# Gating the attention output in three groups, and a fifth pair of weight places for the output projection

## The chip, the cores and the metric

The kernel runs on 1 core of one Trainium2 chip. The metric is the device time of one execution in microseconds (us); lower is better. Engines are named as the profile names them: PE (TensorE) does the matmuls, ACT (ScalarE) and DVE (VectorE) the elementwise work, POOL (GpSimd) and SP (SyncE) little else than issuing DMAs. Each engine works through its own queue strictly in order and waits at semaphores for the others.

## What is computed

Three transformer-like blocks in a row over 256 tokens of 1024 features, all float32. The first block ends in a mixture of 16 experts, whose weights must be streamed from memory. The change concerns the second block, two layers of gated attention:

```python
def second_block(x, norm_g, w_in_a, sinks_a, w_in_b, w_out, final_g):
    h = x
    for i in range(2):
        hn = rmsnorm_2(h, norm_g[i])
        q, k, v, z = split_proj(hn, w_in, n_kv)      # layer 0: n_kv 2, layer 1: n_kv 4
        q, k = apply_rope(q, cos, sin), apply_rope(k, cos, sin)
        o = attention(q, k, v)                       # 16 heads of 64
        o = o.reshape(B, S, 1024) * jax.nn.silu(z)   # the gate
        h = h + o @ w_out[i]                         # the output projection
    return rmsnorm_2(h, final_g)
```

Layer 0 attends over a window of 128 tokens and has a sink; layer 1 is plain causal attention, since all 256 tokens are one block. The third block follows; its first step is a feed-forward layer (`ffn00`), whose weights are 11 chunks of 2 x 256 columns.

## The kernel before

Activations lie feature-major: 8 feature blocks f of 128 features (partitions) by 256 tokens. Float32 accuracy comes from splitting both operands of a matmul into a rounded part and its remainder ("hi" and "lo") and doing three matmuls, hi*hi, hi*lo, lo*hi (L578, L579, L580 in `t_three`). ACT makes the hi of a thing, DVE then subtracts it for the lo.

**Weights.** SP loads them in pieces of 1 MB (256 columns by 1024 rows) into four staging slots, in the order in which they are used (L509). A slot is loaded again once ACT and DVE have split what is in it. The split halves go to a *pair* of places, `WH[j]` and `WL[j]`; there are four pairs, of which the second block uses 0 and 1 in turn. A piece is split in two halves h of 512 rows, each an ACT instruction of 128x1024 (L540 in `a_hi`) and a DVE instruction of 128x1024 (L551 in `v_lo`). Splitting half h of a piece has to wait until PE has used half h of the piece that the pair held (`pair_free`). `a_ahead(q)` and `v_ahead(q)` split pieces q and q+1, if they are not split yet, so that a piece is split one ahead of the chunk that uses it.

**One layer.** The pieces are qa, k, qb, v, qc (2), z (4), o (4). The 8 pairs of heads i are woven with the last two pieces of q and the four of z by `weave`, which fixes the order of every queue when the program is built. For a pair i: PE writes scores (L1158); DVE adds the mask and takes the maximum (L1115, L1128), ACT exponentiates (L1053), DVE normalizes (L1084, L1089); PE transposes the maps (L1005); ACT copies them to SBUF (L1041, `places`); PE multiplies by the values (L1171); ACT copies the result to block i of `qb` (L1179, `out`). For chunk c of z (blocks 2c and 2c+1): PE multiplies, DVE scales by the norm (L2120), ACT takes the tanh (L2007), and DVE finishes the silu (L2112), the last at the next chunk.

**The gate** comes when the attention of all eight pairs is done. It goes block by block: DVE multiplies block f by the gate (L2138), ACT makes its hi (L928), DVE its lo (L2141), and only then does DVE take the next block:

```python
            for f in range(8):
                ...
                for w in self.Vw.new(*self.over("att" + n)):
                    e.wait_ge(*w)
                e.scalar_tensor_tensor(out=q, in0=q, scalar=0.5, in1=F(self.zb)[:, f, :], op0=ALU.mult, ...)
                for w in self.Vw.new(self.act.val(("gated" + n, "h", f))):
                    e.wait_ge(*w)
                e.tensor_tensor(lo, q, f_(F(self.zp[0])[:, f, :]), ALU.subtract)
```

**The output projection** has four chunks c of two 128-row tiles i. A chunk is 48 matmuls of 256 columns in the order: rows' half h, then tile i, then block k = 4h to 4h+3, three matmuls each. So chunk 0 needs the gated blocks 0 to 3 for its first 12 matmuls, again for the next 12, and blocks 4 to 7 in the second half. After a chunk DVE adds the residual (L1541); for the norm that follows, ACT makes the hi of the new blocks times the gain (L1849) and squares them (L882), and DVE makes the lo (L1857) and in layer 1 a copy times the gain (L2149). PE sums the squares (L873) in two parts, blocks 0 to 5 within chunk 3 and the last two blocks in the next work that follows. In layer 1 that is the first chunk of `ffn00`: a tile of 12 matmuls of 512 columns, the squares, then the rest. Its matmuls take the pieces `ffn00.in` (pair 0) and `ffn00.in`+1 (pair 1) side by side.

**Between the layers** the next first piece (qa1, or `ffn00.in`) is split with chunk 3 of the projection; the one behind it (k1, or `ffn00.in`+1) shares pair 1 with the last piece of o, and is split by hand after the last residual and norm steps, around the loading of the table for the square root (L753). The unit numbers of the places: pair j is units 4j and 4j+1 (hi) and 4j+2 and 4j+3 (lo). Units 12, 13 and 16, 17 hold, in the second block, the block's input x and a scratch for its squares.

## Time and profile before

| | before |
|---|---|
| three runs | 2803.73 us median (2801.77 to 2806.78) |
| the profiled execution | 2804.14 us, its span 2802.1 us |
| PE busy, of the span | 2345.7 us, 84% |
| DVE busy | 1227.8 us, 44% |
| ACT busy | 932.8 us, 33% |
| second block, in the span | about 1364 to 1623 us |
| third block | about 1623 to 2802 us |

The first block takes about half the span, most of it streaming expert weights, where DMA is the bound. From 1364 us on PE is busy nearly all the time, and a microsecond matters only where PE waits. The profiled execution was 0.41 us above the median. In a row of the timeline the bracket at the end says how long the engine sat idle before it and who released it; in a row of windows the number ahead of the last two is the granted TensorE clock as a share of full speed, 1.00 for 2.4 GHz and 0.50 for 1.2 GHz.

### The profile page before, as it was taken

To read this page: it belongs to the slowest core of one execution; us is meant where nothing else is said; L and a number is where in the kernel's file an instruction comes from. 1 tells how busy PE (TensorE), PEld (TensorE's weight loads), DVE (VectorE), ACT (ScalarE), POOL (GpSimd) and SP (SyncE) were. 2 spreads that over 40 slices of the span, in tenths; PEclk is the share of its full clock that TensorE was granted. 3 is DMA by queue.
4 is the path that set the end of the run, shared out by engine and by line. 5 is a ranking of instruction groups with operands and counts; after the bars stand their busy time and mean duration, and the time that the engine had idled before them with its cause. 6 is when DMAs were issued, how large, how long until landed. Compare 5 with 4: busy or idle time off the path is not lost.

```text
span 2802.1 us, 37705 instructions
## 1 busy us (share of the span) xinstructions
PE 2345.7 (84%) x16482; PEld 1675.2 (60%) x16482; DVE 1227.8 (44%) x1751; ACT 932.8 (33%) x1524; POOL 61.2 (2%) x36
## 2 busy tenths in 40 slices
PE   8999998656665665566889899999999999977998
PEld 8897784111211121111668778888787888876787
DVE  5567562000100010000476755576656547744654
ACT  5556541000000000000455544354444444632442
POOL 0000010000000000000000000000000000041000
PEclk9999999878888788877989999999999999999999
DMA  7543469999999999999624265575555653412552
GB/s 237 171 157 117 139 209 418 428 428 428 427 428 428 427 428 427 428 428 428 236 76 148 96 198 191 178 241 195 180 181 185 195 206 106 155 34 77 185 191 91
DMA packets 248645, 695.46 MB, mean 248 GB/s; under 512 B 11648, under 2 KB 191104, under 8 KB 222112
## 3 DMA queue, kind: packets, MB, share of 16 engines
q1 hardware_dynamic: 246176, 679.16, 63.7%
q0 software_dynamic: 2016, 13.67, 1.4%
q8 instruction: 130, 2.13, 0.3%
q14 instruction: 35, 0.29, 0.0%
q10 hardware_dynamic: 288, 0.22, 0.0%
HBM read 691.96 MB, written 1.05 MB: 247 GB/s over the span
## 4 chain that ended last, share of the span: by engine, by line
PE 57%; DMA 29%; DVE 8%; ACT 3%; issue 2%; SPq 1%; POOL 0%; DVEq 0%; ACTq 0%
PE ps L578 15%; PE ps L580 15%; PE ps L579 15%; DMA af<-in_w_exp_up 15%; DMA af<-in_w_exp_gate 7%; DMA af<-in_w_exp_down 6%; PE ps L1654 2%; DVE ar L551 2%; PE ps L2594 1%; SPq L509 1%; PE ps L873 1%; PE ps L1684 1%; ACT af L1053 1%; PE ps L2189 1%; DVE af L1089 1%
## 5 line engine op out<-in xcount | busy, mean ns | idle before, releaser
L578 PE MATMUL ps<-ar 128*128 128x512 f32 (+2 forms) x2648 | 928.0, 350 | 27.8 <-DVE ar L551 7.4
L580 PE MATMUL ps<-ar 128*128 128x512 f32 (+2 forms) x2648 | 909.6, 344 | 0.0
L579 PE MATMUL ps<-ar 128*128 128x512 f32 (+2 forms) x2648 | 909.6, 343 | 0.0
L551 DVE TENSOR_TENSOR ar<-af,ar 128x1024 fp32r<-128x1024 f32 x516 | 604.3, 1221 | 290.3 <-ACT ar L540 290.2
L578 PEld LDWEIGHTS ps<-ar 128*128 128x128 f32 x2648 | 504.2, 190 | 104.9 <-issue 11.6
L540 ACT ACTIVATE ar<-af 128x1024 fp32r<-128x1024 f32 x516 | 511.3, 1047 | 164.5 <-PE ps L580 149.1
L580 PEld LDWEIGHTS ps<-ar 128*128 128x128 f32 x2648 | 504.5, 191 | 59.2
L579 PEld LDWEIGHTS ps<-ar 128*128 128x128 f32 x2648 | 505.0, 191 | 56.2 <-issue 0.5
L1654 PE MATMUL ps<-af 128*32 128x512 f32 x2048 | 325.5, 769 | 233.3 <-DMA af<-in_w_exp_up 126.8
L1654 PEld LDWEIGHTS ps<-af 128*32 128x32 f32 x2048 | 63.6, 126 | 480.1 <-DMA af<-in_w_exp_up 199.5
L1823 DVE TENSOR_TENSOR af<-af,ps 128x512 f32<-128x512 f32 x16 | 11.0, 687 | 541.0 <-ACT af L1730 541.0
L1684 PE MATMUL ps<-af 128*32 128x512 f32 x1024 | 168.9, 790 | 93.8 <-DMA af<-in_w_exp_down 82.4
L1730 ACT ACTIVATE af<-ps 128x512 f32<-128x512 f32 x16 | 9.6, 597 | 593.6 <-PE ps L1654 593.6
L1541 DVE TENSOR_TENSOR af<-ps,af 128x512 f32<-128x512 f32 x76 | 48.5, 684 | 299.6 <-PE ps L1696 270.3
L1684 PEld LDWEIGHTS ps<-af 128*32 128x32 f32 x1024 | 35.2, 129 | 210.2 <-DMA af<-in_w_exp_down 140.3
L1737 ACT ACTIVATE af<-ps 128x512 f32<-128x512 f32 x16 | 9.6, 597 | 269.1 <-PE ps L1684 269.1
L2249 DVE TENSOR_TENSOR af<-af,ps 128x256 f32<-128x256 f32 x66 | 27.8, 421 | 125.0 <-ACT af L2220 124.9
L2220 ACT ACTIVATE af<-ps 128x256 f32<-128x256 f32 x66 | 25.3, 384 | 135.7 <-PE ps L580 135.7
L1053 ACT ACTIVATE af<-af,sm 128x256 f32<-128x256 f32 (+1 forms) x136 | 64.0, 474 | 17.1 <-DVE sm L1136 10.2
L2594 PE MATMUL ps<-af 64*64 64x64 f32 x2304 | 44.3, 229 | 20.8 <-issue 16.7
L2594 PEld LDWEIGHTS ps<-af 64*64 64x64 f32 x2304 | 41.2, 141 | 24.5 <-issue 20.0
L2211 ACT ACTIVATE ar<-ps 128x512 fp32r<-128x512 f32 x44 | 26.3, 598 | 81.6 <-PE ps L2189 81.6
(313 smaller groups left out, 1634.8 us busy)
## 6 DMA issues: line engine op xcount, KB each, us to landing
af<-in_w_exp_gate SPq DMA_DIRECT2D x64, 2048.0 KB, 41.2
af<-in_w_exp_up SPq DMA_DIRECT2D x64, 2048.0 KB, 40.8
af<-in_w_exp_down SPq DMA_DIRECT2D x63, 2048.0 KB, 41.5
af<-in_ffn_w_in SPq DMA_DIRECT2D x88, 1024.0 KB, 5.8
af<-in_ffn_w_out SPq DMA_DIRECT2D x44, 1024.0 KB, 5.1
af<-in_w_in SPq DMA_DIRECT2D x34, 1024.0 KB, 5.2
af<-in_sgu_w_in SPq DMA_DIRECT2D x16, 1024.0 KB, 7.0
af<-in_w_out SPq DMA_DIRECT2D x12, 1024.0 KB, 5.3
```

The costliest lines, as they stand in the source:

```text
L509: e.dma_start(view(base), src).then_inc(*(self.row_in[r] if q == self.tail else self.landed[load.slot]).one())
L540: e.activation(self.WH[load.pair][:, c], self.base(i)[:, c], ACT.Copy).then_inc(*self.act.inc(("hi", i, h)))
L551: e.tensor_tensor(self.WL[load.pair][:, c], self.base(i)[:, c], f_(self.WH[load.pair][:, c]), ALU.subtract).then_inc(*self.dve.inc(("lo", ...
L578: e.matmul(o, lh, rh, start=start, stop=False, skip_group_check=True)
L579: e.matmul(o, lh, rl, start=False, stop=False, skip_group_check=True)
L580: return e.matmul(o, ll, rh, start=False, stop=stop, skip_group_check=True)
L873: m = e.matmul(self.bank(name)[:, 0:T], self.C("ones"), F(tmp)[:, f, :], start=first and n == 0, stop=last and n == len(fs) - 1, skip_grou ...
L1053: e.activation(d, d, ACT.Exp, bias=st[:, g:g + 1], accum_out=st[:, 4 + g:5 + g]).then_inc(*self.act.inc((name, "e", i, g)))
L1541: e.tensor_tensor(d, it(self.bank((name, c))), d, ALU.add).then_inc(*self.dve.inc(("out", name, c)))
L1654: t = e.matmul(ps[32 * j:32 * j + 32, bb, :], XE[:, k, c:c + 32], k_(self.base(q), 2)[:, r, 512 * j:512 * j + 512], start=k == 0, stop=k == 7)
L1684: t = e.matmul(ps[o:o + 32, b, :], self.AT_[x % 2][:, r * P + 32 * j:r * P + 32 * j + 32], k_(self.base(q), 4)[:, r, 512 * c:512 * c + 512 ...
L2594: t = e.matmul(self.ps[64 * r:64 * r + 64, banks[n], 64 * c:64 * c + 64], left(tt, h, i, cp), right(tt, h, i, cp), start=True, stop=True)
```

## The change

1. There is a fifth pair, number 4, in units 12, 13 and 16, 17. The four pieces of o take the pairs 4, 0, 1, 4 instead of 0, 1, 0, 1; qa1 and k1, and `ffn00.in` and the piece behind it, take 0 and 1 as before. The first piece of o waits for the last read of x.
2. The first piece of o is split with the last piece of z, one chunk earlier than before.
3. The eight blocks are gated in the groups 0-1, 2-3, 4-5 and 6-7: per group two gates, two hi, two lo. The groups 0-1 and 2-3 stand ahead of the last pair's result in ACT's queue; the last z chunk's work stands between them; `places` for the last pair comes behind the hi of blocks 0-1 and ahead of the last tanh.
4. The piece behind the next first piece is split in chunk 3 of the projection, ahead of the last residual, and DVE makes the lo of the previous blocks ahead of the residual of a chunk, not behind it.

Nothing is computed otherwise: the same instructions stand in another order, and PE's and SP's queues keep theirs.

```diff
@@ -257,7 +257,7 @@
         self.row_in = [Landed(sem("last_row%d_landed" % r)) for r in range(4)]
         self.stored = sem("output_stored")
 
-        self.WH, self.WL = [self.R_(4 * j, 2) for j in range(4)], [self.R_(4 * j + 2, 2) for j in range(4)]
+        self.WH, self.WL = [self.R_(u, 2) for u in (0, 4, 8, 12, 12)], [self.R_(u, 2) for u in (2, 6, 10, 14, 16)]
         self.XP = (self.R_(8, 2), self.R_(10, 2))
         sm = self.sm
         self.SINK, self.NSINK = sm[:, 0:32], sm[:, 288:320]
@@ -396,12 +396,14 @@
         slots[:], count[0] = range(4), 0
         for l in range(2):
             src, nkv = (A["w_in_a_2"], 2) if l == 0 else (A["w_in_b_2"], 4)
+            over_pairs(0, 1)
             columns("qa%d" % l, src, 0, 256)
             columns("k%d" % l, src, 1024, 64 * nkv)
             columns("qb%d" % l, src, 256, 256)
             columns("v%d" % l, src, 1024 + 64 * nkv, 64 * nkv)
             columns("qc%d" % l, src, 512, 512)
             columns("z%d" % l, src, 1024 + 128 * nkv, 1024)
+            over_pairs(4, 0, 1, 4)
             columns("o%d" % l, A["w_out_2"][l], 0, 1024)
         ffn("ffn00", 0, 0)
         over_pairs(0, 1, 2, 3)
@@ -465,6 +467,8 @@
             return [self.pe.val(("raw", self.expert_last[4 * self.loads[q].pair]))]
         if q in stage:
             return self.over(stage[q])
+        if q == at["o0"]:
+            return [self.dve.val(("final1", "o", 7))]
         if 0 <= q - at["rwkv.o"] < 4:
             return [[self.pe.val(("ps", "Gt", 5, 1, 1))], [self.pe.val(("ps", "W2", 1, 1))], [self.pe.val("chunks"), self.pool.val("vb0")],
                     [self.pe.val("chunks")]][q - at["rwkv.o"]]
@@ -1030,7 +1034,7 @@
     def PT(self):
         return self.ptw[:, :].rearrange("p (m c) -> p m c", m=2)
 
-    def a_attention(self, e, name, n, sink, maps, out, causal=False):
+    def a_attention(self, e, name, n, sink, maps, out, causal=False, gated=None):
 
         at = self.rows_of(causal)
 
@@ -1061,6 +1065,9 @@
                 out(e, i - 1)
                 yield
         yield
+        if gated:
+            gated(places)
+            return
         places(n - 1)
         yield
         out(e, n - 1)
@@ -2009,11 +2016,25 @@
             def dense_z():
                 yield from dense_q()
                 yield
-                yield from self.a_proj(e, "z" + n, 4, tanh_z)
-            weave(self.a_attention(e, "att" + n, 8, l == 0, 2, self.a_pv_pair("att" + n, lambda i: F(self.qb)[:, i, :]), True),
-                  dense_z(), 26, 16)
+                for c in range(3):
+                    self.a_ahead(e, self.at["z" + n] + c)
+                    if c == 2:
+                        self.a_ahead(e, self.at["z" + n] + 3)
+                    yield
+                    tanh_z(e, "z" + n, c)
+                    yield
+
+            def gated(fs):
+                self.a_split(e, "gated" + n, self.qb, self.zp, lambda f: [dve.val(("z", n, f))], fs)
+            out, last = self.a_pv_pair("att" + n, lambda i: F(self.qb)[:, i, :]), []
+            weave(self.a_attention(e, "att" + n, 8, l == 0, 2, out, True, last.append), dense_z(), 26, 16)
+            gated((0, 1))
+            last[0](7)
+            tanh_z(e, "z" + n, 3)
+            gated((2, 3))
+            out(e, 7)
             self.end(act, "att" + n)
-            self.a_split(e, "gated" + n, self.qb, self.zp, lambda f: [dve.val(("z", n, f))])
+            gated((4, 5, 6, 7))
             after, hi = ("final2", self.H3[0]) if l else ("norm21", self.H[0])
             gain = (lambda f: self.V("final_g_2", f)) if l else (lambda f: self.V("norm_g_2", 8 + f))
 
@@ -2024,14 +2045,12 @@
             def chunk(e, name, c):
                 if c:
                     gained(c - 1)
+                if c == 3:
+                    self.a_ahead(e, self.at["ffn00.in"] if l else self.at["qa1"])
             run(self.a_proj(e, "o" + n, 4, chunk))
             self.end(act, "layer" + n)
             gained(3)
-            second = (self.at["ffn00.in"] + 1) if l else self.at["k1"]
-            self.a_hi(e, second, 0)
             self.a_sqrt_table(e)
-            self.a_hi(e, second, 1)
-            self.a_next = second + 1
         self.end(act, "final2")
 
     def v_second(self, e):
@@ -2126,19 +2145,39 @@
                 yield from dense_q()
                 rope("q" + n, F(self.qb), 3)
                 yield
-                yield from self.v_proj(e, "z" + n, 4, silu_z)
-                silu_last("z" + n, 3)
+                for c in range(3):
+                    self.v_ahead(e, self.at["z" + n] + c)
+                    yield
+                    silu_z(e, "z" + n, c)
+                    if c == 2:
+                        self.v_ahead(e, self.at["z" + n] + 3)
+                    yield
+
+            def gate(*fs):
+                for f in fs:
+                    q = F(self.qb)[:, f, :]
+                    for w in self.Vw.new(self.act.val(("att" + n, "o", f)), dve.val(("out", "z" + n, f // 2))):
+                        e.wait_ge(*w)
+                    e.scalar_tensor_tensor(out=q, in0=q, scalar=0.5, in1=F(self.zb)[:, f, :], op0=ALU.mult, op1=ALU.mult).then_inc(*dve.inc(("z", n, f)))
+
+            def gate_lo(*fs):
+                for f in fs:
+                    for w in self.Vw.new(self.act.val(("gated" + n, "h", f))):
+                        e.wait_ge(*w)
+                    e.tensor_tensor(F(self.zp[1])[:, f, :], F(self.qb)[:, f, :], f_(F(self.zp[0])[:, f, :]), ALU.subtract).then_inc(*dve.inc(("gated" + n, "l", f)))
             weave(self.v_attention(e, "att" + n, 8, lambda i: [(self.C("mb") if l else self.C("ma"), 1.0)], sink=None if l else 16, causal=True),
                   dense_z(), 26, 16)
+            gate(0, 1)
+            gate_lo(0, 1)
+            silu_z(e, "z" + n, 3)
+            gate(2, 3)
+            silu_last("z" + n, 3)
+            gate_lo(2, 3)
             self.end(dve, "att" + n)
-            for f in range(8):
-                q, lo = F(self.qb)[:, f, :], F(self.zp[1])[:, f, :]
-                for w in self.Vw.new(*self.over("att" + n)):
-                    e.wait_ge(*w)
-                e.scalar_tensor_tensor(out=q, in0=q, scalar=0.5, in1=F(self.zb)[:, f, :], op0=ALU.mult, op1=ALU.mult).then_inc(*dve.inc(("z", n, f)))
-                for w in self.Vw.new(self.act.val(("gated" + n, "h", f))):
-                    e.wait_ge(*w)
-                e.tensor_tensor(lo, q, f_(F(self.zp[0])[:, f, :]), ALU.subtract).then_inc(*dve.inc(("gated" + n, "l", f)))
+            gate(4, 5)
+            gate_lo(4, 5)
+            gate(6, 7)
+            gate_lo(6, 7)
             after, lo = ("final2", self.H3[1]) if l else ("norm21", self.H[1])
             gain = (lambda f: self.V("final_g_2", f)) if l else (lambda f: self.V("norm_g_2", 8 + f))
             residual = self.v_residual(F(self.x2))
@@ -2149,16 +2188,14 @@
                     e.tensor_scalar(F(self.B(6))[:, f, :], F(self.x2)[:, f, :], gain(f), None, ALU.mult).then_inc(*dve.inc((after, "u", f)))
 
             def chunk(e, name, c):
-                residual(e, name, c)
                 if c:
                     gained(c - 1)
+                if c == 3:
+                    self.v_ahead(e, self.at["ffn00.in"] if l else self.at["qa1"])
+                residual(e, name, c)
             run(self.v_proj(e, "o" + n, 4, chunk))
             self.end(dve, "layer" + n)
             gained(3)
-            second = (self.at["ffn00.in"] + 1) if l else self.at["k1"]
-            self.v_lo(e, second, 0)
-            self.v_lo(e, second, 1)
-            self.v_next = second + 1
         self.end(dve, "final2")
```


The queues at three places, before and then after. In the changed program the lines read L544 for L540 (hi of weights), L555 for L551 (lo of weights), L932 for L928, L2161 for L2138, L2167 for L2141 (hi, gate and lo of a block), L1045 for L1041 (`places`), L1186 for L1179 (`out`), L2014 for L2007 (tanh), L2139 for L2120 (scaling), L2131 for L2112 (silu), L1548 for L1541 (residual), L1864 for L1857 and L2188 for L2149 (lo and copy for the norm).

ACT in layer 0, from the exponentials of the last pair to the first piece of the projection that it splits behind the gate (before):

```order
L1058 ACTIVATE sm<-sm 128x4
L540 ACTIVATE ar<-af 128x1024 [waits slot2_landed]
L540 ACTIVATE ar<-af 128x1024
L1179 ACTIVATE af<-ps 128x256 [waits tensor_wrote]
L2007 ACTIVATE af<-af 128x512 [waits vector_wrote]
L1041 ACTIVATE af<-ps 128x384 [waits tensor_wrote] x2
L1179 ACTIVATE af<-ps 128x256 [waits tensor_wrote]
L928 ACTIVATE ar<-af 128x256 [waits vector_wrote] x8
L540 ACTIVATE ar<-af 128x1024 [waits slot3_landed]
```

The same place, after:

```order
L1062 ACTIVATE sm<-sm 128x4
L1186 ACTIVATE af<-ps 128x256 [waits tensor_wrote]
L932 ACTIVATE ar<-af 128x256 [waits vector_wrote] x2
L1045 ACTIVATE af<-ps 128x384 [waits tensor_wrote] x2
L2014 ACTIVATE af<-af 128x512 [waits vector_wrote]
L932 ACTIVATE ar<-af 128x256 [waits vector_wrote] x2
L1186 ACTIVATE af<-ps 128x256 [waits tensor_wrote]
L932 ACTIVATE ar<-af 128x256 [waits vector_wrote] x4
L544 ACTIVATE ar<-af 128x1024 [waits slot3_landed]
```

The split of o's first piece (the two L540 at the top) is gone from here to a place one chunk earlier, the hi of the gated blocks is cut in 2, 2 and 4, and `places` (L1041) stands ahead of the tanh (L2007).

DVE in layer 0, from the end of the last pair's normalizing (before):

```order
L1089 TENSOR_SCALAR af<-af,sm 128x256
L551 TENSOR_TENSOR ar<-af,ar 128x1024 [waits scalar_wrote,slot2_landed]
L551 TENSOR_TENSOR ar<-af,ar 128x1024 [waits scalar_wrote]
L2120 TENSOR_TENSOR af<-ps,sm 128x512 [waits tensor_wrote]
L2112 SCALAR_TENSOR_TENSOR af<-af 128x512
L2112 SCALAR_TENSOR_TENSOR af<-af 128x512 [waits scalar_wrote]
L2138 SCALAR_TENSOR_TENSOR af<-af 128x256 [waits vector_wrote,gpsimd_wrote,scalar_wrote,tensor_wrote]
L2141 TENSOR_TENSOR ar<-af,ar 128x256 [waits scalar_wrote]
L2138 SCALAR_TENSOR_TENSOR af<-af 128x256
L2141 TENSOR_TENSOR ar<-af,ar 128x256 [waits scalar_wrote]
```

The same place, after:

```order
L1096 TENSOR_SCALAR af<-af,sm 128x256
L2161 SCALAR_TENSOR_TENSOR af<-af 128x256 x2
L2167 TENSOR_TENSOR ar<-af,ar 128x256 [waits scalar_wrote] x2
L2139 TENSOR_TENSOR af<-ps,sm 128x512 [waits tensor_wrote]
L2131 SCALAR_TENSOR_TENSOR af<-af 128x512
L2161 SCALAR_TENSOR_TENSOR af<-af 128x256 x2
L2131 SCALAR_TENSOR_TENSOR af<-af 128x512 [waits scalar_wrote]
L2167 TENSOR_TENSOR ar<-af,ar 128x256 [waits scalar_wrote] x2
L2161 SCALAR_TENSOR_TENSOR af<-af 128x256 [waits vector_wrote]
L2161 SCALAR_TENSOR_TENSOR af<-af 128x256
L2167 TENSOR_TENSOR ar<-af,ar 128x256 [waits scalar_wrote] x2
```

The lo of o's first piece (the two L551) is gone from here, and the gates go in twos around the last two pieces of z work, with no wait for the end of the attention ahead of the first four.

DVE in layer 1, the last steps up to the reciprocal of the third block's first norm (before):

```order
L1541 TENSOR_TENSOR af<-ps,af 128x512 [waits tensor_wrote]
L1857 SCALAR_TENSOR_TENSOR ar<-af,vec,ar 128x256 [waits scalar_wrote] x2
L2149 TENSOR_SCALAR af<-af,vec 128x256 x2
L1857 SCALAR_TENSOR_TENSOR ar<-af,vec,ar 128x256 [waits scalar_wrote] x2
L2149 TENSOR_SCALAR af<-af,vec 128x256 x2
L551 TENSOR_TENSOR ar<-af,ar 128x1024 [waits scalar_wrote,slot1_landed]
L551 TENSOR_TENSOR ar<-af,ar 128x1024 [waits scalar_wrote]
L905 RECIPROCAL sm<-sm 128x256 [waits scalar_wrote]
```

The same place, after:

```order
L1864 SCALAR_TENSOR_TENSOR ar<-af,vec,ar 128x256 [waits scalar_wrote] x2
L2188 TENSOR_SCALAR af<-af,vec 128x256 x2
L555 TENSOR_TENSOR ar<-af,ar 128x1024 [waits scalar_wrote,slot1_landed]
L555 TENSOR_TENSOR ar<-af,ar 128x1024 [waits scalar_wrote]
L1548 TENSOR_TENSOR af<-ps,af 128x512 [waits tensor_wrote]
L1864 SCALAR_TENSOR_TENSOR ar<-af,vec,ar 128x256 [waits scalar_wrote] x2
L2188 TENSOR_SCALAR af<-af,vec 128x256 x2
L909 RECIPROCAL sm<-sm 128x256 [waits scalar_wrote]
```

The lo of the piece behind `ffn00.in` (slot1) and the lo of blocks 4 and 5 now stand ahead of the last residual (L1541, now L1548) and not behind it.

## Rows read from the trace of the kernel before

**Rows 1.** The waits of PE from 1450 to 1500 us: total, times, longest.

```profile
PE ps L1171 <- ACT af L1041: 4.5, 2, 3.0
PE ps L578 <- DVE ar L2141: 3.4, 5, 2.0
```

**Rows 2.** Windows: length, PE, PEld, DVE, ACT, POOL busy, clock, DMA share, GB/s.

```profile
1456.00:1474.00 18.00, 11.57 (x65) 9.57 (x63) 11.29 (x23) 8.13 (x16) 0.00 (x0) 0.72 0.17 58
...
1582.00:1599.00 17.00, 11.15 (x61) 9.32 (x59) 10.49 (x22) 7.75 (x15) 0.00 (x0) 0.70 0.19 63
...
1619.00:1634.00 15.00, 10.52 (x40) 8.70 (x41) 8.87 (x14) 8.61 (x12) 1.23 (x2) 0.77 0.38 121
1634.00:2802.00 1168.00, 1108.37 (x8508) 937.01 (x8506) 692.13 (x856) 518.65 (x710) 47.63 (x22) 0.99 0.49 164
```

**Rows 3.** Timeline of DVE, layer 0: start us, us, line, operation, tiles.

```profile
1453.56 0.16 DVE L1081 TENSOR_TENSOR sm<-sm 128x4 f32<-128x4 f32 x1 [2.69 <-ACT sm L1058]
...
1454.90 2.35 DVE L551 TENSOR_TENSOR ar<-af,ar 128x1024 fp32r<-128x1024 f32 x2
1457.17 0.68 DVE L2120 TENSOR_TENSOR af<-ps,sm 128x512 f32<-128x512 f32 x1
1457.77 1.47 DVE L2112 SCALAR_TENSOR_TENSOR af<-af 128x512 f32<-128x512 f32 x2
1461.39 0.42 DVE L2138 SCALAR_TENSOR_TENSOR af<-af 128x256 f32<-128x256 f32 x1 [2.15 <-ACT af L1179]
1462.30 0.43 DVE L2141 TENSOR_TENSOR ar<-af,ar 128x256 fp32r<-128x256 f32 x1 [0.48 <-ACT ar L928]
1462.64 0.42 DVE L2138 SCALAR_TENSOR_TENSOR af<-af 128x256 f32<-128x256 f32 x1
...
1471.01 0.42 DVE L2141 TENSOR_TENSOR ar<-af,ar 128x256 fp32r<-128x256 f32 x1 [0.48 <-ACT ar L928]
```

**Rows 4.** Timeline of ACT, layer 0.

```profile
1450.30 0.63 ACT L2007 ACTIVATE af<-af 128x512 f32<-128x512 f32 x1 [4.50 <-DVE af L2120]
...
1461.85 0.42 ACT L928 ACTIVATE ar<-af 128x256 fp32r<-128x256 f32 x1 [0.55 <-DVE af L2138]
```

**Rows 5.** Timeline of PE, layer 0.

```profile
1459.33 1.55 PE L1171 MATMUL ps<-af 128*64 128x256 f32 x8 [2.99 <-ACT af L1041]
...
1471.58 0.36 PE L578 MATMUL ps<-ar 128*128 128x256 f32 x1 [0.65 <-DVE ar L2141]
```

**Rows 6.** Timeline of DVE, layer 1.

```profile
1580.48 2.35 DVE L551 TENSOR_TENSOR ar<-af,ar 128x1024 fp32r<-128x1024 f32 x2
...
1596.39 0.42 DVE L2141 TENSOR_TENSOR ar<-af,ar 128x256 fp32r<-128x256 f32 x1 [0.48 <-ACT ar L928]
```

**Rows 7.** Issues of o's weights on SP (first and last start), then time to landing.

```profile
L509 SPq DMA_DIRECT2D af<-in_w_out x4: 367/367/368, 1410.8 to 1447.4; - x4
...
DMA to landing us min/median/max: 5.0/5.1/6.4
```

**Rows 8.** Timeline of PE, from the end of layer 1 into the third block.

```profile
1618.57 0.28 PE L580 MATMUL ps<-ar 128*128 128x256 f32 x1
1623.48 0.77 PE L578 MATMUL ps<-ar 128*128 128x512 f32 x1 [4.64 <-DVE ar L551]
...
1628.74 1.41 PE L873 MATMUL ps<-af,cst 128*128 128x256 f32 x4
1629.81 0.58 PE L578 MATMUL ps<-ar 128*128 128x512 f32 x1
...
1631.82 0.39 PE L580 MATMUL ps<-ar 128*128 128x512 f32 x1
```

**Rows 9.** Timeline of DVE at the same place.

```profile
1618.88 0.69 DVE L1541 TENSOR_TENSOR af<-ps,af 128x512 f32<-128x512 f32 x1 [4.06 <-PE ps L580]
```

**Rows 10.** Timeline of ACT at the same place.

```profile
1620.42 0.61 ACT L882 ACTIVATE af<-af 128x512 f32<-128x512 f32 x1
```

**Rows 11.** Window in layer 1, with the columns of rows 2.

```profile
1540.00:1545.00 5.00, 2.72 (x18) 1.32 (x18) 3.85 (x6) 1.49 (x4) 0.00 (x0) 1.00 0.36 125
```

## Prediction

> **What bounds the kernel now.** I read the page for the shares first: PE is busy for 84% of the span, so the second and third blocks should be read by PE's waits. The windows say where they are [rows 2]: in the third block PE is busy 1108 of 1168 us, but in 1456 to 1474 it is busy 11.57 of 18, in 1582 to 1599 11.15 of 17, in 1619 to 1634 10.52 of 15, and in these three alone the clock is at 0.7 to 0.8. They are the hand-over from attention to projection in layer 0 and layer 1, and from the projection to the third block. A wait there delays all that follows: PE, the bound of what comes after, starts later by as much, and no load runs ahead of it (SP loads a slot only after a split, and the splits follow PE).
>
> What PE waits for in layer 0: for `places` of the last pair (L1041; 4.5 us in two waits, 3.0 the longest), then for gated blocks (L2141; 3.4 us in five waits) [rows 1]. The timelines show why. DVE is done with normalizing at 1454.90, makes the lo of o's first piece, and scales the last z chunk only at 1457.17 [rows 3]. ACT's tanh waits for that, `places` stands behind the tanh, and PE's last value matmuls begin at 1459.33 instead of right behind their transposes [rows 5]. Then all eight blocks are gated by a ping-pong of DVE and ACT, a round each: first gate 1461.39, first lo 1462.30, last lo 1471.01 [rows 3]: 8.71 us for seven rounds, 1.24 us a round. PE can't finish the first projection chunk before the last lo, and resumes for block 7 at 1471.58 [rows 5]. So the place that decides is the time from the end of normalizing to the last lo: 16.11 us in layer 0, and 1580.48 to 1596.39, 15.91 us, in layer 1 [rows 3, 6].
>
> **Part 1: gating in groups.** No instruction is added or removed, so I walk DVE's new queue with steps from before. Steps: a 256-column operation to the next, 0.34 (1462.30 to 1462.64); a 512-column one, 0.60 (1457.17 to 1457.77); gate to hi 0.46 (1461.39 to 1461.85) and hi to lo 0.45 (1461.85 to 1462.30) [rows 3, 4]. From 1454.90: gates 0 and 1 at 0 and 0.34; their hi at 0.46 and 0.80 on ACT; lo 0 and 1 at 0.91 and 1.25; scaling of the last z 1.59; silu of the third chunk 2.19; gates 2, 3 at 2.79 and 3.13; the last silu 3.47; lo 2, 3 at 4.07 and 4.41; gates 4, 5 at 4.75 and 5.09; lo 4, 5 at 5.66 and 6.00; gates 6, 7 at 6.34 and 6.68; lo 6, 7 at 7.25 and 7.59. The last lo begins 7.59 us after normalizing instead of 16.11: **8.5 us** in layer 0, and 15.91 - 7.59 = **8.3 us** in layer 1.
>
> What must not come late for this: (a) The last silu needs the last tanh, and this the scaling. Before, the two silus behind the scaling run from 1457.77 to 1459.24, the second 0.68 of it, so it began by 1458.56, 1.39 us after the scaling's start [rows 3]; in the walk that would be 1.59 + 1.39 = 2.98, ahead of the 3.47 at which DVE comes to it. (b) `places` now stands behind the hi of blocks 0 and 1, which ends at about 1.2, that is 1456.1, and PE's last transposes end at 1459.33 - 2.99 = 1456.34 [rows 5]; so nothing but the copy itself lies between them and the values, which start at about 1457. (c) Gates 6 and 7 need the result of these values at 6.34. Even at the 1.55 us of before [rows 5] they end at 1458.6, and `out` behind them by 1459.1, that is 4.2. (d) PE has the 33 matmuls ahead of block 7 done in time: they take about 4 us at full rate, and block 2's lo comes over 3 us ahead of block 7's. PE therefore still waits in the first chunk, but for about 1 us at a time, and the last lo decides, as before.
>
> **Part 2: o's first piece split earlier.** Two ACT instructions (2.0 us) and two of DVE (2.3 us) move one chunk forward. ACT sits idle 4.50 us ahead of the tanh at 1450.30 [rows 4], and DVE idle 2.69 us ahead of 1453.56 [rows 3], exactly where they now stand: DVE's cover is 0.4 us larger than what is put in it. Where that cover fails, all behind it slips by the excess. The piece has long landed: o's four were issued from 1410.8 to 1447.4 and land in 5 to 6.4 us [rows 7]. Its pair is new, so no use by PE has to be waited for, and the last read of x was made early in the attention. I cost it at nothing; bounds: 0 to +0.4 us a layer, from the two idle times. Behind it on SP stands the load of the next first piece, which is issued some 4 us earlier, into idle DMA engines (share 0.17 and 0.19 in the two windows [rows 2]).
>
> **Part 3: the last splits in chunk 3.** Before, PE ends the last projection chunk with a start at 1618.57 and waits until 1623.48 for the lo of the piece behind `ffn00.in` (4.64 us), because its split stands behind the residual (1618.88), two steps of the norm and the table load. After so long a wait the clock is at the lower level: twelve matmuls of 512 columns take 1623.48 to 1628.74, 0.438 us each, against 0.223 each in the nine starts from 1629.81 to 1631.82 [rows 8, 9]. Afterwards this pair is free once chunk 2 is done, since o's last piece is in pair 4. From then PE has chunk 3 and twelve squares matmuls to do, 48 x 0.112 + 12 x 0.17 or more, at least 7.4 us (0.112 is half of 0.223; 0.17 a quarter of the 0.7 below), and DVE, the fuller of the two, a residual of 0.7, two pieces of 2.35, lo and copies of 1.3, 6.7 us in all (four steps of 0.34 for lo and copies) [rows 3, 9]. So PE goes on at about 1618.7: twelve matmuls at 0.223 bring it to 1621.4, the four squares matmuls take about 0.7 (1.07 at mostly the lower level, so between 0.5 and 1.1), and the second dozen begins at 1622.1 instead of 1629.81: **7.7 us**. Next late there is the square of the last blocks, done at 1621.03 [rows 10], 0.3 us ahead of need. Between layers 0 and 1 the same edit brings nothing: PE has another 24 matmuls of qa1 and no wait there.
>
> **Sum.** 8.5 + 8.3 + 7.7 = 24.5 us. Against the profiled execution's own 2804.14 this gives 2779.6; that execution was 0.4 above the median of its three, so I give 2779.5. The bound of the moved work (0.4 a layer) and of the squares (0.4) leave 22.9 to 25; the three runs of before lie 5 us apart, which adds 2.5 either way.
>
> **The rivals.**
>
> *The clock falls although the waits are shorter* (12%). PE still stops and starts between gated blocks. If it is at half rate there, the 27 matmuls between blocks 2 and 7 take 27 x 0.22 = 5.9 us (half of 0.438 for 256 columns) where 3.5 are to be had, so PE comes 2.4 us late to block 7, and the last 15 cost 1.6 more: 4 us a layer, 2783.5 for one and 2787.5 for both. Against it: in layer 1 PE was idle 2.28 of 5 us in several waits and the clock stayed at 1.00 [rows 11]; it fell only where a single wait was 2 us or longer (2.99 in [rows 5], 4.64 in [rows 8]), and I expect none above 1.1. The Trainium skill speaks for this rival: "TensorE: Matmul & The Clock Gate", in "A second HAM failure mode: psum-queue depth-cycling", says that short idle times between groups of matmuls can make the clock swing between its two levels, which by its own measure would spoil the first chunk of both layers; by that rule the time is the 2787.5 above, and the window just named is against it.
>
> *The hole at the third block stays* (7%). The new split stands ahead of the last residual in DVE's queue. If it waits there for anything of chunk 3's time, the residual and everything behind it come late, and the wait and the low clock come back in another form: 24.5 - 7.7 = 16.8 us gained, 2787.3. For it: DVE's queue is in order, the residual is what the norm waits for. Against: the 6.7 in 7.4 us worked out above, though that is close.
>
> *The cover fails in the attention* (6%): DVE comes late to the normalizing of the last pair, `places` and the last values slip, and of each 8.4 only half is left, 2788.
>
> *Slower* (2%): the clock stays at the lower level not for a chunk but through both projections, since the stop-and-go now begins earlier and nothing long follows to lift it. Each of their 384 matmuls of 256 columns then costs 0.107 us more (half of 0.438 - 0.223): +41 us, 2820. It decides from 24.5 / 0.107 = 229 such matmuls on. Against it: before, after a wait of 2.99 and five smaller, the clock was at 1.00 again within a chunk (0.72 on average over the window [rows 2]).
>
> *The forecast as worked out*: 70%; the last 3% for what I don't see.
>
> **How the numbers follow.** The forecast alone reaches from 2776.5 to 2783.5. The rivals on the fast side end at 2788, with 25% together, so the range is 2776 to 2788. A measurement of this kernel tells 0.2%, 5.6 us, from no change. All cases but the slower one and part of the unseen lie over 15 us below: faster 0.95, same 0.03, slower 0.02.
>
> **What would show it.** Right, step by step: from the end of DVE's last normalizing to the start of the last lo 7.6 us (now 16) in both layers; the last value matmuls 0.6 us behind their transposes; no wait of PE over 1.1 us between them and chunk 1, and a clock of 1.00 there; no wait of PE between the last projection matmul and the first of the third block, whose first dozen takes 2.7 us; the third block as long as before, 1109 us busy. Wrong: a PE wait for L555 (splits) in chunk 0 or 3 (then a cover was misjudged); a clock at 0.5 in the first chunk (first rival); the walk right but the total short of it (then the third block waits for loads).

## The result: 25 us less, and the profile after

The changed kernel takes 2777.36 us (median of 4, 2776.71 to 2778.70), the kernel before 2802.75 us (median of 4, 2801.71 to 2806.78). The ratio is 0.9908, with a 95% interval of 0.9896 to 0.9921. The forecast was 2779.5 us in a range of 2776 to 2788, so it was right; it is 2.1 us off, less than the 0.2% that a measurement here can tell. Two executions in a slower state, 2889.01 us of the gating alone and 4476.28 us of a kernel before, are in the medians below but not in the ratios. The profiled execution took 2778.70 us, with a span of 2776.7 us.

Line numbers have moved: L582 to L584 are the projections' matmuls (L578 to L580 before), L544 and L555 the hi and lo of the weights (L540, L551), L2161 and L2167 the gate and its lo (L2138, L2141), L1045 `places`, L1178 the values, L2139 and L2131 the scaling and silu of z.

The waits of PE from 1450 to 1500 us, which answer [rows 1] (total, times, longest):

```profile
PE ps L1178 <- ACT af L1045: 2.0, 2, 1.4
PE ps L582 <- DVE ar L2167: 0.8, 1, 0.8
```

7.9 us of waiting have become 2.8. The windows at the same three places, shifted to where they now lie, answer [rows 2] (length, PE, PEld, DVE, ACT, POOL, clock, DMA share, GB/s):

```profile
1456.00:1474.00 18.00, 16.55 (x136) 15.65 (x135) 15.58 (x29) 13.54 (x25) 0.00 (x0) 1.00 0.49 163
1574.00:1591.00 17.00, 15.83 (x130) 14.93 (x129) 15.26 (x28) 12.82 (x23) 0.00 (x0) 1.00 0.48 158
1602.50:1617.50 15.00, 15.00 (x77) 12.51 (x76) 10.48 (x15) 10.90 (x16) 1.23 (x2) 1.00 0.82 290
```

PE does 136 matmuls in the first 18 us where it did 65, at a clock of 1.00 where it had 0.72, and the third window has no idle time left. The timeline of DVE in layer 0 answers [rows 3]: o's lo in the idle time, then the first two gates, and the last two low parts (a group's second operation starts 0.34 us after the first). The blocks are gated in four groups of two; the three of the title are the 2, 2 and 4 blocks in which ACT makes the hi.

```profile
1451.52 2.35 DVE L555 TENSOR_TENSOR ar<-af,ar 128x1024 fp32r<-128x1024 f32 x2
1454.30 0.16 DVE L1088 TENSOR_TENSOR sm<-sm 128x4 f32<-128x4 f32 x1 [0.42 <-ACT sm L1062]
...
1455.63 0.75 DVE L2161 SCALAR_TENSOR_TENSOR af<-af 128x256 f32<-128x256 f32 x2
...
1462.84 0.76 DVE L2167 TENSOR_TENSOR ar<-af,ar 128x256 fp32r<-128x256 f32 x2
```

and in layer 1 [rows 6]:

```profile
1572.64 0.76 DVE L2161 SCALAR_TENSOR_TENSOR af<-af 128x256 f32<-128x256 f32 x2
...
1579.85 0.76 DVE L2167 TENSOR_TENSOR ar<-af,ar 128x256 fp32r<-128x256 f32 x2
```

From the end of normalizing to the start of the last lo: 1462.84 + 0.34 - 1455.63 = 7.55 us, and 1579.85 + 0.34 - 1572.64 = 7.55 us. The walk had 7.59. PE in layer 0 [rows 5]: the values start 0.63 us behind their transposes, and one wait is left in the first chunk.

```profile
1457.71 0.87 PE L1178 MATMUL ps<-af 128*64 128x256 f32 x8 [0.63 <-ACT af L1045]
...
1460.25 0.36 PE L582 MATMUL ps<-ar 128*128 128x256 f32 x1 [0.76 <-DVE ar L2167]
```

PE at the hand-over to the third block [rows 8]: the first dozen of 512 columns follows the last projection matmul at once, at the upper clock level, and the second dozen starts at 1605.93.

```profile
1602.38 0.28 PE L584 MATMUL ps<-ar 128*128 128x256 f32 x1
1602.50 0.40 PE L582 MATMUL ps<-ar 128*128 128x512 f32 x1
...
1605.25 1.02 PE L877 MATMUL ps<-af,cst 128*128 128x256 f32 x4
1605.93 0.58 PE L582 MATMUL ps<-ar 128*128 128x512 f32 x1
```

**Where the time went.** ScalarE loads the exponentials' table at the start of each layer's attention and the silu's at the start of the third block. These are landmarks that every version has; the first three rows are of the kernel before, the others of the changed one:

```profile
1391.00 1.28 ACT L1053 ACT_TABLE_LOAD   x1
...
1522.04 1.28 ACT L1053 ACT_TABLE_LOAD   x1
...
1636.44 1.28 ACT L2220 ACT_TABLE_LOAD   x1
```

```profile
1391.74 1.28 ACT L1057 ACT_TABLE_LOAD   x1
...
1514.22 1.28 ACT L1057 ACT_TABLE_LOAD   x1
...
1612.60 1.28 ACT L2257 ACT_TABLE_LOAD   x1
```

Stage A (layer 0 from its attention on, to layer 1's attention) went from 131.04 to 122.48 us, 8.56 less. Stage B (from there to the third block's silu) went from 114.40 to 98.38, 16.02 less. Together 24.58, against a forecast of 24.5. The span fell by 25.4 us: the attention of layer 0 begins 0.74 later, and what follows the last landmark (the "rest") is 1.56 shorter (1164.10 for 1165.66 us). The change touches nothing there; that difference is treated below.

### The profile page after: what moved, and what is told of

Its sections match the earlier page's. It is cut to its first block, busy times and chain, and to the rows that moved or that the text cites. A ratio compares the mean times of both kernels' runs of the same rounds, so it can differ in the third digit from the quotient of the medians.

```text
span 2776.7 us, 37696 instructions
## 1 busy us (share of the span) xinstructions
PE 2339.0 (84%) x16482; PEld 1668.4 (60%) x16482; DVE 1227.0 (44%) x1751; ACT 931.3 (34%) x1524; POOL 61.2 (2%) x36
## 4 chain that ended last, share of the span: by engine, by line
PE 58%; DMA 29%; DVE 8%; ACT 3%; issue 1%; SPq 1%; POOL 0%; ACTq 0%; DVEq 0%
PE ps L582 16%; PE ps L584 15%; PE ps L583 15%; DMA af<-in_w_exp_up 13%; DMA af<-in_w_exp_gate 9%; DMA af<-in_w_exp_down 6%; PE ps L1661 2%; DVE ar L555 1%; PE ps L2631 1%; SPq L513 1%; PE ps L877 1%; PE ps L1691 1%; ACT af L1057 1%; PE ps L2226 1%; DVE af L1096 1%
## 5 line engine op out<-in xcount | busy, mean ns | idle before, releaser
L582 PE MATMUL ps<-ar 128*128 128x512 f32 (+2 forms) x2648 | 925.1, 349 | 17.6 <-DVE ar L3276 2.9
L584 PE MATMUL ps<-ar 128*128 128x512 f32 (+2 forms) x2648 | 907.2, 343 | 0.0
L555 DVE TENSOR_TENSOR ar<-af,ar 128x1024 fp32r<-128x1024 f32 x516 | 604.2, 1221 | 288.3 <-ACT ar L544 288.2
L544 ACT ACTIVATE ar<-af 128x1024 fp32r<-128x1024 f32 x516 | 510.4, 1047 | 158.8 <-PE ps L584 142.5
L582 PEld LDWEIGHTS ps<-ar 128*128 128x128 f32 x2648 | 502.2, 190 | 93.3 <-issue 12.0
L584 PEld LDWEIGHTS ps<-ar 128*128 128x128 f32 x2648 | 502.2, 190 | 59.1
L1548 DVE TENSOR_TENSOR af<-ps,af 128x512 f32<-128x512 f32 x76 | 48.6, 685 | 296.1 <-PE ps L1703 273.5
```

The costliest lines, as they stand in the source:

```text
L544: e.activation(self.WH[load.pair][:, c], self.base(i)[:, c], ACT.Copy).then_inc(*self.act.inc(("hi", i, h)))
L555: e.tensor_tensor(self.WL[load.pair][:, c], self.base(i)[:, c], f_(self.WH[load.pair][:, c]), ALU.subtract).then_inc(*self.dve.inc(("lo", ...
L582: e.matmul(o, lh, rh, start=start, stop=False, skip_group_check=True)
L584: return e.matmul(o, ll, rh, start=False, stop=stop, skip_group_check=True)
L1548: e.tensor_tensor(d, it(self.bank((name, c))), d, ALU.add).then_inc(*self.dve.inc(("out", name, c)))
```

## The experiments

In the thirteen traces the rest is 1154.7 to 1165.7 us long, though no edit touches it. So an edit in the second block is read from the two stages of its trace, and the medians only check it. How far this can be trusted was tried too. (What the expectations call head 6 and head 7 are the last two of the eight pairs of heads, pairs 6 and 7.)

> The changed kernel once more, as it is, beside the other runs of this set. Theory: the two stages of the second block are as long as in the first trace of it (122.48 and 98.38 us between the loads of ScalarE's tables at the starts of the two attentions and at the third block's first silu) within 0.3 us, and the difference to the first trace lies in the third block, which no step of the change touches: there the clock of TensorE falls behind waits of 1.6 to 2.4 us in some executions and not in others. Rival: the second block itself varies by a microsecond and more, so that the edits' sizes read from single traces would be uncertain by as much.

Measured: stages of 122.47 and 98.36 us, 0.01 and 0.02 from the first trace; the rest 1162.9 for 1164.1 us. Its median was 2774.44 us, with 2797.38 us for the kernel before beside it (ratio 0.9915, 0.9901 to 0.9928). These two traces speak against the rival. But in four of the thirteen traces the clock falls early in layer 1's attention, at a place that no edit touches, and stage B is 0.3 to 1.7 us longer for it (58.70 to 60.12 us from the attention's start to the end of normalizing, where the nine others have 58.4 or, with the tanh late, 58.0). So 0.1 us means something only once that part is looked at, as is done below.

All versions (us; "before beside it" is the kernel before on the same chip; "early" and "late" name the two later ones):

| kernel | stage A | stage B | rest | median | before beside it | ratio, 95% |
|---|---|---|---|---|---|---|
| before | 131.04 | 114.40 | 1165.7 | 2802.75 | | |
| changed | 122.48 | 98.38 | 1164.1 | 2777.36 | 2802.75 | 0.9908 (0.9896-0.9921) |
| changed again | 122.47 | 98.36 | 1162.9 | 2774.44 | 2797.38 | 0.9915 (0.9901-0.9928) |
| gating alone | 122.48 | 105.97 | 1159.7 | 2780.73 | 2800.49 | 0.9933 (0.9915-0.9951) |
| hand-over alone | 131.05 | 106.95 | 1160.0 | 2790.28 | 2800.49 | 0.9968 (0.9956-0.9981) |
| four pairs | 124.35 | 102.06 | 1158.7 | 2778.82 | 2800.49 | 0.9926 (0.9910-0.9942) |
| o's split late | 124.92 | 100.79 | 1154.7 | 2779.29 | 2800.49 | 0.9935 (0.9914-0.9957) |
| one at a time | 127.56 | 104.23 | 1162.4 | 2786.97 | 2800.86 | 0.9951 (0.9937-0.9966) |
| twos, all behind | 125.99 | 101.62 | 1159.5 | 2780.97 | 2797.38 | 0.9941 (0.9927-0.9954) |
| two products more | 123.61 | 99.99 | 1161.6 | 2781.01 | 2800.86 | 0.9930 (0.9916-0.9945) |
| four products more | 126.41 | 102.85 | 1161.1 | 2783.55 | 2800.86 | 0.9938 (0.9923-0.9953) |
| gates early | 121.73 | 97.92 | 1164.8 | 2775.43 | 2800.86 | 0.9907 (0.9891-0.9924) |
| and tanh late | 121.06 | 97.23 | 1158.5 | 2770.70 | 2797.38 | 0.9900 (0.9887-0.9914) |

**The two halves, each alone.** First the gating with the old end of the layer (DVE's side):

```diff
+                residual(e, name, c)
                 if c:
                     gained(c - 1)
-                if c == 3:
-                    self.v_ahead(e, self.at["ffn00.in"] if l else self.at["qa1"])
-                residual(e, name, c)
...
             gained(3)
+            second = (self.at["ffn00.in"] + 1) if l else self.at["k1"]
+            self.v_lo(e, second, 0)
+            self.v_lo(e, second, 1)
```

> The changed kernel, but with the steps at the end of each layer in the order of the kernel before: the piece behind the next first piece is split after the last residual and norm steps, and the residual stands ahead of the lo of the blocks before. The fifth pair stays. Theory (the order made the hole at the third block, not the pair): PE's wait of about 4.6 us for the lo and the twelve matmuls at the lower clock come back, the two gains in the attention (8.6 and 8.4 us) stay: 2777.4 + 7.7 = 2785 us. Rival (the free pair is what closed the hole): no wait over 1 us there, 2777 us.

Measured: stage A as changed to the hundredth, stage B 7.59 us longer. PE's wait and the twelve matmuls at the lower level are both back, with the fifth pair in place (timeline of PE, then its window):

```profile
1606.60 0.77 PE L582 MATMUL ps<-ar 128*128 128x512 f32 x1 [4.64 <-DVE ar L555]
```

```profile
1606.60:1611.90 5.30, 5.30 (x13) 4.19 (x14) 1.23 (x1) 0.97 (x2) 0.00 (x0) 0.50 0.32 108
```

So the order of the splits made this hole, and it costs nothing between layers 0 and 1. Then the pair and the new end, with the old gating and o's first split at its old place:

```diff
             self.end(dve, "att" + n)
-            gate(4, 5)
-            gate_lo(4, 5)
...
+            for f in range(8):
+                gate(f)
+                gate_lo(f)
```

> The other half: fifth pair and new order at the end of each layer, but the gating of the kernel before (all eight blocks after the attention, gate, hi, lo one block at a time, o's first piece split after the last normalizing). Theory: the halves add up, so 2802.8 - 7.7 = 2795 us, with the waits for places (about 3 us) and gated blocks back in both layers. Rival (the handover only pays because the clock comes through high from the gating part): under 5 us gained, 2798 us or more.

Measured: stage A as before, stage B 7.45 us shorter. The gating alone took 8.56 and 8.43 us off the two stages and the hand-over on top of it 7.59; alone the hand-over took 7.45, so the halves add to 0.14 us. These 0.14 don't lie in the hand-over: from layer 1's last lo to the third block's silu it is 32.40 us for 40.05, 7.65 less, but the old walk in layer 1 was 16.11 us here for 15.91. By the medians they don't: the halves are worth 19.8 and 10.2 us, 30.0 together, and the whole 25.4 and 22.9 in its two sets. The expected 2785 and 2795 us were missed by 4 to 5 us. The rests of these two traces, 1159.7 and 1160.0 us for 1164.1, are about as much shorter, and the intervals of the ratios (13.7 to 23.8 and 5.3 to 12.3 us) hold the 16.8 and 7.7 forecast.

**The fifth pair.** o's four pieces lie in the four old pairs, as before:

```diff
-            over_pairs(4, 0, 1, 4)
             columns("o%d" % l, A["w_out_2"][l], 0, 1024)
...
-        if q == at["o0"]:
-            return [self.dve.val(("final1", "o", 7))]
```

> The changed kernel without the fifth pair: the four pieces of o take pairs 0, 1, 0, 1 again, in the new order. Theory (the pair is needed for the hand-over alone): the split of the second half of the next piece has to wait for the last matmul of the projection and now stands ahead of the residual, so residual and squares come about 2.3 us later, and PE waits about 1.6 us for the squares in each layer: 2777.4 + 3.3 = 2780.7 us; the gating part is untouched. Rival 1 (the hole comes back whole): 2785 us. Rival 2 (o's first piece can't be split early either without the pair, and the gating part loses 2 us a layer as well): 2785 us, but with the last lo of the gate over 9 us behind the normalizing.

Measured: 1.87 us more in stage A and 3.68 in stage B. The first is close to what was expected: PE waits 1.59 us for the squares, because ACT can round the next piece only when its pair is free, and the squares stand behind it. The walk is 7.55 us in both layers here too, so o's first piece is split early without the pair as well, and rival 2 is out. The second contains the same wait,

```profile
1611.40 1.13 PE L874 MATMUL ps<-af,cst 128*128 128x256 f32 x4 [1.73 <-ACT af L883]
```

and something that has nothing to do with pairs. Early in layer 1's attention PE's clock fell, behind a wait of 1.65 and one of 0.64 us. These two waits, and the two before them, stand in all thirteen traces to within 0.02 us, and in the changed kernel's two the clock stayed up (timeline and window of this version):

```profile
1539.69 1.55 PE L1175 MATMUL ps<-af 128*64 128x256 f32 x8 [0.64 <-ACT af L1042]
```

```profile
1539.60:1543.00 3.40, 3.31 (x10) 1.27 (x10) 1.19 (x5) 2.07 (x10) 0.00 (x0) 0.50 0.00 0
```

(The same eight matmuls take 0.87 us in the changed kernel.) So the pair's own worth is about 1.9 us a layer (1.86 and 1.99 behind the last lo), and 1.7 of the 5.5 us is a fall of the clock that no edit explains. The median, 2778.82 us, grew by only 1.5; the rest of this trace is 5.4 us shorter than in the changed kernel's.

**o's first split.** `a_ahead` and `v_ahead` of z + 3 stand behind the third chunk again (DVE's side):

```diff
                     silu_z(e, "z" + n, c)
-                    if c == 2:
-                        self.v_ahead(e, self.at["z" + n] + 3)
                     yield
+                self.v_ahead(e, self.at["z" + n] + 3)
+                yield
```

> The changed kernel, but o's first piece is split where the kernel before did it, behind the last normalizing on DVE and the last exponentials on ACT, ahead of the first gates. Theory (DVE's walk from the end of normalizing to the last lo decides): the two lo of 128x1024 put 2.3 us into the walk, 7.6 becomes 9.9 us, so 2777.4 + 4.6 = 2782 us; since places comes behind it too, PE waits 2.9 us and the clock may fall, which adds up to 4 us. Rival (the grouping alone made the gain, and the split hides behind PE): 2777 to 2778 us.

Measured: 2.44 and 2.41 us. DVE is idle for 2.69 us again ahead of pair 7's normalizing and makes the 2.35 us of lo behind it. PE's wait for `places` is 2.85 us, and the values run at the lower level behind it:

```profile
1458.98 1.55 PE L1178 MATMUL ps<-af 128*64 128x256 f32 x8 [2.85 <-ACT af L1045]
```

**Twos or place?** The gating edit does two things: it takes two blocks at a time, and it puts half of them ahead of the last values. First twos undone, place kept:

```diff
-            gate(0, 1)
-            gate_lo(0, 1)
+            def one_by_one(*fs):
+                for f in fs:
+                    gate(f)
+                    gate_lo(f)
+            one_by_one(0, 1)
```

> The changed kernel, but the feature blocks are gated one at a time: gate 0, low part of 0, gate 1, low part of 1, and so on, in the same places of VectorE's order (blocks 0 to 3 still stand ahead of the last values). Theory: with two blocks at once the two engines work in turn without a stop; one at a time VectorE has to wait for ScalarE's rounding of each block, about 0.47 us, eight times. The walk from the first gate to the last low part grows from 7.55 us to about 11.5 us, so each of the two layers takes 3.9 us longer than in the changed kernel and the whole about 7.7 us. Rival: only the place ahead of the last values brings the gain, and TensorE has other work while VectorE walks; then the layers grow by under 1 us each. Second rival: the order of twos is worth its full 3.9 us only in the part behind the last values (4 blocks, 1.9 us a layer), since ahead of them VectorE is waited for by nobody.

Measured: 5.08 and 5.85 us longer, more than expected (0.7 of the 5.85 is the early part of layer 1's attention, where PE's clock fell as it did with four pairs). The walk is right: DVE waits 0.48 us for each block's hi (one row shown),

```profile
1457.04 0.43 DVE L2167 TENSOR_TENSOR ar<-af,ar 128x256 fp32r<-128x256 f32 x1 [0.48 <-ACT ar L932]
```

and the last lo starts at 1467.55, 11.41 us behind normalizing. What comes on top is the clock. PE has five waits in the first chunk, none over 0.66 us (waits of PE from 1455 to 1500), and with the fifth it falls; the last longer wait, 1.48 us for `places`, had ended 8 us earlier:

```profile
PE ps L582 <- DVE ar L2167: 3.1, 5, 0.7
```

```profile
1465.00:1468.00 3.00, 1.18 (x6) 0.83 (x6) 1.95 (x5) 1.34 (x4) 0.00 (x0) 0.93 0.00 0
1468.00:1472.00 4.00, 3.88 (x22) 3.91 (x23) 2.91 (x3) 3.31 (x4) 0.00 (x0) 0.63 0.00 0
```

Then place undone, twos kept: ACT does `places(7)`, the tanh and `out(7)` first, and all four twos stand behind them.

```diff
-            gate(0, 1)
-            gate_lo(0, 1)
             silu_z(e, "z" + n, 3)
-            gate(2, 3)
             silu_last("z" + n, 3)
-            gate_lo(2, 3)
...
+            for f in (0, 2, 4, 6):
+                gate(f, f + 1)
+                gate_lo(f, f + 1)
```

> The changed kernel with the blocks gated two at a time, but all of them behind the attention's last output, as in the kernel before. It tells the two halves of the gating edit apart. Theory, walked through with the durations of the changed kernel's trace: the last output is copied about 3.4 us after the normalizing of head 7 ends, the four twos take 0.9 + 3 x 1.57 + 0.34 us from there, so that the last low part starts about 9.4 us behind the normalizing instead of 7.55 us, and each layer is about 1.9 us longer than in the changed kernel, 3.8 us in all, if TensorE's waits for the low parts (about 2.1 and 0.9 us) leave its clock up. Rival: the place is worth more than the twos, 4 us a layer or more, because TensorE sits idle longer at the projection's start and its clock falls.

Measured: 3.51 and 3.24 us longer. The walk again is as worked out in layer 0 (9.39 us for 9.4; in layer 1 it is 9.69, where DVE also waits 1.03 us for z's sums), and again the clock adds to it, here behind a wait of 1.94 us:

```profile
1460.08 0.56 PE L582 MATMUL ps<-ar 128*128 128x256 f32 x1 [1.94 <-DVE ar L2165]
```

```profile
1460.00:1464.00 4.00, 3.92 (x17) 3.73 (x18) 3.71 (x11) 1.71 (x5) 0.00 (x0) 0.50 0.00 0
```

**A longer wait, put in.** Products of 128x512 that nobody reads, between the last silu and the lo of blocks 2 and 3:

```diff
             silu_last("z" + n, 3)
+            for i in range(2):
...
+                e.tensor_tensor(self.th[0], self.cst[:, 0:512], self.cst[:, 0:512], ALU.mult).then_inc(*dve.inc(("filler" + n, i)))
             gate_lo(2, 3)
```

> The changed kernel with two needless VectorE products over 128x512 (they write a table that nobody reads any more) between the silu of the last feature pair and the low parts of blocks 2 and 3, in both layers. TensorE's wait for those low parts was 0.76 us in layer 0 and 0.47 us in layer 1. Each product is about 0.65 us, 1.3 us for the two. Theory: the walk of VectorE sets the end of the gating, so each layer grows by about 1.3 us, TensorE waits 2.1 and 1.8 us, and 2.6 us are lost in all. Rival by the clock: with a wait of about 2 us TensorE's clock falls ahead of the output projection, and each layer grows by 1.5 us or more on top, 5.5 us or more in all. Rival by slack: VectorE has room there, and less than 0.5 us a layer is lost.

> As the run with two needless products, but with four of them, about 2.6 us a layer. Theory: TensorE waits 3.4 us in layer 0 and 3.1 us in layer 1, each layer grows by 2.6 us, 5.2 us in all, if the clock stays. The kernel before showed waits of 2.99 and 4.64 us at two places with a fall of the clock behind them, so here a fall is likelier than not: then 1.5 to 4 us more in each layer, 8 to 13 us in all. Which of the two comes tells whether the length of the single wait decides the fall.

Measured with two: PE waits 2.09 and 1.75 us, stage A is 1.13 and stage B 1.61 us longer, and the clock stays up behind them (timeline and window, layer 0). The walk is 1.33 us longer in both layers; layer 0's attention was 0.2 us shorter than in the changed kernel, and layer 1's 0.3 longer, by the early fall of the clock told above.

```profile
1461.87 0.36 PE L582 MATMUL ps<-ar 128*128 128x256 f32 x1 [2.09 <-DVE ar L2167]
```

```profile
1461.00:1465.00 4.00, 3.10 (x24) 2.93 (x25) 3.70 (x11) 1.75 (x5) 0.00 (x0) 1.00 0.00 0
```

With four: waits of 3.54 and 3.25 us, stages 3.93 and 4.47 us longer, of which the walk has 2.77 and 2.78, and the clock falls in both layers (1.2 us each; the other 0.5 of stage B is the early part of the attention again):

```profile
1462.98 0.56 PE L582 MATMUL ps<-ar 128*128 128x256 f32 x1 [3.54 <-DVE ar L2167]
```

```profile
1463.00:1467.00 4.00, 4.00 (x21) 4.00 (x22) 3.12 (x10) 2.63 (x6) 0.00 (x0) 0.59 0.00 0
```

In shorter windows, the clock is at the lower level up to 1466.3 and at the upper one from there:

```profile
1463.00:1466.30 3.30, 3.30 (x15) 3.30 (x16) 3.01 (x9) 1.93 (x5) 0.00 (x0) 0.50 0.00 0
1466.30:1468.00 1.70, 1.70 (x17) 1.70 (x16) 1.11 (x2) 1.70 (x3) 0.00 (x0) 1.00 0.00 0
```

The last lo starts at 1465.91, so only 0.4 us of the low clock lie behind it, and the fall costs 1.2 us all the same: PE started a matmul only every 0.22 us in these 3.3 us, instead of every 0.12, and came late to the last blocks.

**The walk as a ledger.** Layer 0 of these versions, from the timelines of DVE and the landmarks:

| kernel | normalizing to last lo | last lo to layer 1's attention | clock |
|---|---|---|---|
| before | 16.11 | 51.03 | low up to 1469, then up |
| changed (both traces) | 7.55, 7.54 | 51.04, 51.04 | up |
| two products more | 8.87 | 51.03 | up |
| o's split late (walk with the 2.3 of lo) | 9.82 | 51.18 | low up to 1462.2, then up |
| gates early / and tanh late | 6.78 / 6.63 | 51.05 / 51.05 | up |
| four products more | 10.32 | 52.21 | low from 1462.9 to 1466.3 |
| one at a time | 11.41 | 52.28 | low from 1467.6 to 1471.0 |
| twos, all behind | 9.39 | 52.72 | low from 1459.3 to 1466.1 |

In the rows without a fall that PE feels, what follows the last lo is 51.03 to 51.05 us whatever the walk was (51.18 with o's split late). The gating alone (7.55 and 51.03) and the hand-over alone (16.11 and 51.04) fit as well; four pairs have 52.89, by PE's wait for the squares. Layer 1 reads likewise, from its last lo to the third block's silu: 32.40 or 32.41 us in the changed kernel's two traces, the hand-over alone, two products more and the two versions with early gates, 32.57 with o's split late, and 33.62, 33.70 and 33.51 in the last three rows. So each microsecond of the walk is one of the kernel, and a fall of the clock that PE feels adds 1.1 to 1.7 us. In the kernel before the clock was at 0.50 for most of the walk (about 10 us, from 1458.8) and back at 1.00 by its end:

```profile
1459.00:1463.00 4.00, 1.68 (x9) 0.93 (x9) 1.36 (x4) 1.07 (x3) 0.00 (x0) 0.50 0.68 238
1463.00:1467.00 4.00, 3.22 (x11) 2.42 (x12) 2.34 (x7) 1.43 (x4) 0.00 (x0) 0.50 0.00 0
...
1471.00:1475.00 4.00, 3.42 (x28) 3.45 (x29) 3.40 (x5) 3.77 (x4) 0.00 (x0) 1.00 0.00 0
```

There it cost nothing: PE was waiting for DVE anyway, and had only slower matmuls in place of idle time.

**A shorter walk.** The first two gates need nothing that is late, and DVE sits idle for 1.82 us ahead of pair 6's normalizing. Put there:

```diff
             yield
+            if i in early:
+                early[i]()
             if causal:
                 normed(i)
```

with `early={6: lambda: gate(0, 1)}`, and `gate(0, 1)` behind the attention left out.

> The changed kernel, but the two gates of blocks 0 and 1 stand on VectorE ahead of the normalizing of head 6, where VectorE sat idle for 1.82 us in layer 0, and no longer behind the normalizing of head 7. Nothing else moves. Theory: they cost nothing there, the walk behind head 7 shrinks by the 0.9 us that they took, and TensorE's wait of 0.76 us in layer 0 and 0.47 us in layer 1 for the low parts of blocks 2 and 3 goes: 0.76 and 0.47 us a layer, 1.2 us in all, since behind that wait TensorE runs without a stop. Rival: the last low part still sets the end, and each layer gives back the whole 0.9 us, 1.8 us in all. Rival against: VectorE is not idle in layer 1 at that place, or the gates hold up the normalizing of head 6, and the layers are as long as they were or longer by up to 0.5 us.

Measured: 0.75 and 0.46 us less; PE's waits for L2167 are gone in both layers. The walk of layer 0 shrinks by 0.77 to 6.78 us, so theory and first rival meet there; in layer 1 DVE now reaches z's last chunk before PE has summed it,

```profile
1573.72 0.69 DVE L2141 TENSOR_TENSOR af<-ps,sm 128x512 f32<-128x512 f32 x1 [0.36 <-PE ps L584]
```

and only 0.46 us are left of the gain: the two engines are even. The next thing ahead of both is ACT's order: the tanh of z's third chunk stands ahead of pair 6's `places` and pair 7's exponentials, and PE waits 1.3 us for the one, DVE 0.4 us for the other. One more `yield` puts the tanh behind both:

```diff
                     yield
+                    if c == 2:
+                        yield
                     tanh_z(e, "z" + n, c)
```

> The kernel with the first two gates ahead of head 6's normalizing, and on top the tanh of z's third pair on ScalarE behind the exponentials of head 7 instead of ahead of head 7's predecessor's places and those exponentials. Theory: behind the normalizing of head 7 VectorE is the engine that sets the end, and it waits 0.42 us in layer 0 and 0.33 us in layer 1 for ScalarE's exponentials of head 7; with the tanh behind them these waits go, and each layer shrinks by about 0.4 and 0.3 us against the kernel with early gates, 0.7 us in all, 1.9 us in all against the changed kernel. TensorE's wait of 1.3 us for head 6's places falls to about 0.7 us, which by itself brings nothing. Rival: that wait of TensorE is on the path too, and the layers shrink by 0.6 us or more each. Rival against: the silu of the third pair is then late and holds VectorE, and nothing is gained.

Measured: 0.67 and 0.69 us less than with early gates, 1.42 and 1.15 less than the changed kernel. That is the rival's size: besides DVE's waits for the exponentials, its wait for z's sums shrinks, since PE gets to them sooner. The median is 2770.70 us (2769.59 to 2771.52) beside 2774.44 us (2773.50 to 2777.23) for the changed kernel on the same chip, the fastest version here. Of these 3.7 us the stages explain 2.6; the rest of the span varies by more than the remaining 1.1.

## Why the prediction was right

*Part 1, gating.* 8.5 and 8.3 us were forecast, 8.56 and 8.43 measured (the second from the gating alone). The step list holds to 0.04 us, and so does the claim that the last lo decides; the ledger shows it for six walks from 6.6 to 16.1 us (0.15 off in one of them), and for three more up to what the clock adds. Of (a) to (d) only the wait in (d) is left, 0.76 and 0.47 us.

*Part 2, o's split.* Costed at nothing, found at nothing: DVE's idle time ahead of pair 7's normalizing went from 2.69 to 0.42 us, and from the attention's start to the end of normalizing it is 63.89 us before and after. Undone, it costs 2.4 us a layer, so it was a condition of the 7.55 us, not an extra.

*Part 3, hand-over.* 7.7 us forecast; the stages give it 7.59 us on top of the gating and 7.45 alone (7.65 without what the walk of layer 1 adds), so the term was at most 0.25 too high. The square of the last blocks was said to be ready 0.3 us ahead of need; ACT ended it 0.4 us ahead (1604.25 and 0.61, against 1605.25):

```profile
1604.25 0.61 ACT L886 ACTIVATE af<-af 128x512 f32<-128x512 f32 x1
```

That close call is what the fifth pair pays for: without it the square comes 1.7 us late.

*The rival of the clock* did not come, but the reason against it was wrong. I wrote that the clock fell only behind a single wait of 2 us or more. It fell behind 1.94 us, behind 1.65 and 0.64, and behind five waits of at most 0.66 us; it stayed up behind 2.09 us. The Trainium skill tells of such a case, of a bf16 kernel that cycles through PSUM banks ("TensorE: Matmul & The Clock Gate", "A second HAM failure mode: psum-queue depth-cycling"): short idle times between groups of matmuls made the clock swing. The version with one block at a time agrees with it: five waits of 0.46 to 0.66 us, and the clock fell to 0.50. So that the clock stayed up in the changed kernel is measured, in two traces, and not explained: on this point the forecast had luck. The price in that rival, 4 us a layer, was too high: 1.1 to 1.7 us were measured. The rival let the low clock last for the whole first chunk, but it lasted 3.3 us with four products more and under 7 us with the twos all behind. Its chance of 12% was not too high: the clock fell, in both layers, in the two versions that undo one half of the gating each.

*The slower rival* (no recovery through both projections) has nothing for it: the longest fall of the clock in the second block, that of the kernel before, was over within 12 us, the others sooner.

*The range.* The bounds named, 0.4 us a layer and 0.4 for the squares, leave 23.3 and not 22.9; the slow side of the forecast was 0.4 us wide of its own sum. On the fast side the range was narrow: in its second set the changed kernel's median was 2774.44 us, below the 2776, with the kernel before at 2797.38 beside it. The difference, 22.9 us, is what can be compared across sets, and with 25.4 in the first it has the 24.5 between them.

*What the sum did not have.* The span fell by 0.9 us more than 24.5. That is +0.74 ahead of the second block's landmarks and -1.56 behind them. The landmarks of the third block (every load of a table on ScalarE) show where the 1.56 lie: its parts agree to 0.1 us between the two traces, but for three. The first became longer. PE waits there for the lo of a piece for 2.24 us before and 2.25 after, the same wait. Before, the clock stayed up behind it (first row), after, it fell (second and third):

```profile
1924.00:1928.00 4.00, 3.86 (x17) 3.17 (x18) 3.49 (x4) 2.31 (x3) 0.00 (x0) 1.00 0.38 97
```

```profile
1900.34 0.79 PE L582 MATMUL ps<-ar 128*128 128x512 f32 x1 [2.25 <-DVE ar L555]
```

```profile
1900.20:1904.20 4.00, 3.86 (x10) 3.10 (x11) 3.50 (x4) 1.60 (x2) 0.00 (x0) 0.57 0.33 98
```

Up to the silu of the feed-forward part behind that wait, seven of the thirteen traces take 341.1 to 341.3 us from the third block's first silu and six take 339.6 to 339.7: a fall or none, 1.6 us. Which it is follows no edit that I can name. So this part cost the changed kernel's execution 1.6 us. The other two parts gave it back twice over, 2.5 us in the stretch between these loads (two rows before, two after) and 0.7 us in the next:

```profile
2420.51 1.28 ACT L2918 ACT_TABLE_LOAD   x1
2567.79 1.28 ACT L2990 ACT_TABLE_LOAD   x1
```

```profile
2398.24 1.28 ACT L2955 ACT_TABLE_LOAD   x1
2543.03 1.28 ACT L3027 ACT_TABLE_LOAD   x1
```

147.28 us became 144.79. In the thirteen traces this stretch takes 138.6 to 147.3 us and the next 46.6 to 49.0, in versions that differ nowhere near, and that is nearly all of the spread of the rest. Its cause stays open. PE's busy time in the third block is as before (1109.3 us for 1108.4). So of the 25.4 us the traces put 24.58 down to the change; the other 0.9 is noise of these two executions.

## To carry to other kernels

Where two engines hand blocks to and fro, write the sequence down with start-to-start steps and read off when the last block is out: that one number was the stage here, to 0.05 us, wherever no fall of the clock came on top. Two blocks at a time fill the partner's latency, and work whose inputs are ready early belongs in the idle time ahead of the last late input. Each counts by itself (127.56 us with the place alone and 125.99 with the twos alone, both with o's first piece split early, for 131.04 before), but with either one missing the clock fell too. Judge such an edit by landmarks around its stage, since a fall of the clock elsewhere moves the total by more than the edit.

## What was not expected of the hardware

The length of a single wait doesn't tell whether TensorE's clock falls. Behind 2.09 us it stayed at 1.00, behind 1.94 us it went to 0.50; behind one and the same pair of waits, 1.65 and 0.64 us early in layer 1, it stayed in nine traces and fell in four (four pairs, one at a time, two and four products more), though what PE waits for in that attention up to there is the same in all to 0.02 us; behind 2.25 us in the third block it fell in seven of thirteen. Behind the waits of 2.85 us and more (2.85, 2.99, 3.25, 3.54, 4.64) it fell each time. A series of waits of 0.66 us was enough for one. What decides between these stays open; the runs with products put in show only that the length alone doesn't.

A low clock cost nothing where TensorE had time to spare. In the kernel before, it lasted for most of a walk of 16 us and left no trace in what followed (51.03 us, as with the clock up). Where blocks came in twos, TensorE had no such time: with four products more, 3.3 us at the lower level made it 1.2 us late, though nearly all of them lay ahead of the last lo.
